# Moving the low halves of the first stream's cached values in a sample-attention loop

## The reference

```python
K = jnp.concatenate([prev_k, k], axis=1)      # 1024 cached + 16 new rows
V = jnp.concatenate([prev_v, v], axis=1)
F = jnp.cumsum(jnp.concatenate([prev_logf, logf], axis=1), axis=1)
s = einsum('bqhd,bkhd->bhqk', q, K) * scale + F_q - F_k
s = where(k_pos <= q_pos, s, -inf)
o = einsum('bhqk,bkhd->bqhd', softmax(s), V)
```

## Time and the profile before

| | |
|---|---|
| time of the runs | 1510.03 us median of 3 (1509.64 to 1511.13) |
| time of the profiled execution | 1514.69 us |
| its span | 1513.0 us |
| PE busy | 1474.3 us, 97% |
| DVE busy | 878.7 us, 58% |
| ACT busy | 616.2 us, 41% |
| POOL busy | 484.4 us, 32% |
| samples' attention | about 1161 to 1340 us of the span |

### The profile page before, as it was taken

How to read it: one execution, slowest core, us unless ns; L and a number is a source line. 1 busy time by engine, 2 the same in 40 slices (tenths; PEclk the granted TensorE clock), 3 DMA queues, 4 the chain that set the end, 5 groups by cost and what they waited for, 6 DMA issues and landing times.

```text
span 1513.0 us, 23830 instructions
## 1 busy us (share of the span) xinstructions
PE 1474.3 (97%) x8828; PEld 1310.5 (87%) x8828; DVE 878.7 (58%) x1883; ACT 616.2 (41%) x1307; POOL 484.4 (32%) x760
## 2 busy tenths in 40 slices
PE   8999999999999999999999999999998999999999
PEld 8997888888889999999888889889887788777887
DVE  4333103343364452321789888988986788798663
ACT  5443112131131110100578778777876444442220
POOL 2110004545540020102465665565573222103221
PEclk9999999999999999999999999999999899999999
DMA  5533114534330020160544853664433566644442
GB/s 165 157 110 100 44 67 127 167 112 143 94 105 27 22 68 20 42 137 24 123 100 83 144 119 65 128 134 81 97 98 129 186 227 229 242 141 151 156 160 91
DMA packets 180116, 174.48 MB, mean 115 GB/s; under 512 B 72543, under 2 KB 138240, under 8 KB 176928
## 3 DMA queue, kind: packets, MB, share of 16 engines
q1 hardware_dynamic: 177488, 163.97, 39.5%
q10 hardware_dynamic: 2448, 8.91, 1.5%
q0 software_dynamic: 64, 0.07, 0.1%
HBM read 123.27 MB, written 49.12 MB: 114 GB/s over the span
## 4 chain that ended last, share of the span: by engine, by line
PE 71%; DVE 9%; POOL 7%; issue 7%; ACT 5%; DMA 1%; DVEq 0%; ACTq 0%; POOLq 0%
PE banks L1069 19%; PE banks L1063 13%; PE banks L2690 7%; PE banks L1646 6%; PE banks L1662 4%; POOL in_h_rstd L589 3%; PE banks L1663 3%; PE banks L1636 3%; PE banks L1637 3%; PE banks L2139 3%; PE banks L2169 3%; POOL in_out L594 3%; ACT pa_s_ring L1528 2%; PE banks L2120 2%; DVE in_out L876 1%
## 5 line engine op out<-in xcount | busy, mean ns | idle before, releaser
L1063 PE MATMUL banks<-in_w_hi,in_xt_hi 128*128 128x512 f32 (+1 forms) x680 | 243.2, 358 | 4.3 <-DVE in_w_lo L767 2.5
L1063 PE MATMUL banks<-in_w_hi,in_xt_lo 128*128 128x512 f32 (+1 forms) x680 | 237.9, 350 | 0.0
L1063 PE MATMUL banks<-in_w_lo,in_xt_hi 128*128 128x512 f32 (+1 forms) x680 | 237.3, 349 | 0.0
L1608 DVE TENSOR_TENSOR pa_pt_lo<-banks,pa_pt_hi 128x512 fp32r<-128x512 f32 (+2 forms) x320 | 192.6, 606 | 20.1 <-ACT pa_pt_hi L1551 19.8
L1551 ACT ACTIVATE pa_pt_hi<-banks 128x512 fp32r<-128x512 f32 (+2 forms) x320 | 165.2, 537 | 86.8 <-PE banks L1646 86.5
L1069 PE MATMUL banks<-in_xt_hi,in_w_hi 128*128 128x384 f32 (+1 forms) x576 | 192.5, 334 | 0.9 <-DVE in_w_lo L773 0.7
L1069 PE MATMUL banks<-in_xt_hi,in_w_lo 128*128 128x384 f32 (+1 forms) x576 | 189.4, 329 | 0.0
L1069 PE MATMUL banks<-in_xt_lo,in_w_hi 128*128 128x384 f32 (+1 forms) x576 | 189.1, 328 | 0.0
L1646 PE MATMUL banks<-ident,pa_s_ring 128*128 128x128 f32 x1088 | 172.9, 274 | 12.6 <-ACT pa_s_ring L1528 7.2
L1528 ACT ACTIVATE pa_s_ring<-pa_s_ring,pa_low 128x1024 f32<-128x1024 f32 (+2 forms) x192 | 173.1, 902 | 0.1
L1662 PE MATMUL banks<-pa_pt_hi,pa_vs 128*128 128x256 f32 x576 | 165.2, 303 | 2.5 <-DVE pa_parts L1590 1.7
(11 more groups left out here) (293 smaller groups left out, 2872.3 us busy)
## 6 DMA issues: line engine op xcount, KB each, us to landing
sa_k_c<-in_cache_k_dram SPq DMA_DIRECT2D x8, 2048.0 KB, 9.8
sa_v_c<-in_cache_v_dram SPq DMA_DIRECT2D x8, 2048.0 KB, 9.4
out_dram<-in_out SPq DMA_DIRECT2D x34, 256.0 KB, 2.1
out_dram<-op_x ACTq DMA_DIRECT2D x17, 512.0 KB, 3.3
scratch_qk_t<-in_t_hi SPq DMA_DIRECT2D x32, 256.0 KB, 2.6
scratch_qk_t<-in_t_lo SPq DMA_DIRECT2D x32, 256.0 KB, 3.0
pa_q_l<-scratch_qk_t SPq DMA_DIRECT2D x16, 512.0 KB, 13.1
pa_ks<-scratch_qk_t SPq DMA_DIRECT2D x16, 512.0 KB, 6.3
```

Source lines behind the costliest of these rows:

```text
L1063: mm = pe.matmul(ps[:, u % NBANK, 0:n], tile_of(xa, t)[:, k, :], wa[:, k, c0:c0 + n], start=(k == 0 and q == 0), stop=(k == KT - 1 and q = ...
L1608: dve.tensor_tensor(pt_lo[g % 2][:, b:b + nb, cols], ps_t[:, turn_use(h, j, n) % 3, 0:nb * P].rearrange("p (b q) -> p b q", q=P), pt_hi[g ...
```

## The change

The four `low_v` calls of stream 0 leave their place behind the row minimum of stream 0. Two of them now stand in stream 1 behind the minimum of chunk 0, and two behind the minimum of chunk 1, each pair ahead of the `low_p(0)` that follows. The `low_v` of streams 1 to 7 stay where they were. ACT waits for the prompt's output stores before its first write of `p_hi`.

```diff
@@ sample_attention, on_act
         def high_p(b, part):
             for n in part:
                 tiles = PB[n]
+                if b == 0 and n == 0:
+                    prompt.stores_landed(act)
                 act.wait_ge(p_turned, b * 3 + n + 1)
@@ sample_attention, on_dve, the loop over streams
             low_k(b, 2)
             minima(b, par, 0)
+            if b == 1:
+                low_v(0, 0, 0)
+                low_v(0, 0, 1)
             if b:
                 low_p(b - 1, (0, 1))
             if b + 1 < NB:
                 low_k(b + 1, 0)
             minima(b, par, 1)
+            if b == 1:
+                low_v(0, 0, 2)
+                low_v(0, 0, 3)
             if b:
                 low_p(b - 1, (2,))
...
             dve.tensor_reduce(low[:, par, 3:4], low[:, par, 0:3], AX_X, ALU.min).then_inc(row_min, 1)
-            for quarter in range(4):
-                low_v(b, par, quarter)
+            if b:
+                for quarter in range(4):
+                    low_v(b, par, quarter)
```

## The result

The changed kernel takes 1530.07 us, median of 4 runs (1527.44 to 1530.75), beside 1510.58 us for the kernel before in its 4 runs (1509.64 to 1512.25). The ratio is 1.0112, 95% interval 1.0095 to 1.0129: slower by 17 us by the ratio, by 19.5 us by the medians. The forecast was 1524.5 us, +14.5 us, in a range of 1519.5 to 1528.5. (The ratio, put on the 1510.03 us from which the forecast started, gives 1526.9 us, inside it.) In another group of runs the same kernel took 1528.87 us against 1512.70 us, ratio 1.0103 (1.0090 to 1.0117), +16.2 us. The profiled executions differ by 16.0 us of span: 1529.0 us after, 1513.0 us before.

The account below looks back on a forecast made before the run. The prediction took PE, busy 97% of the span, to bound the kernel. It added 11.5 us of stall and 3.0 us of slow clock, 14.5 us, to 1510.03 us: 1524.5 us, range 1519.5 to 1528.5 us.

Parts of the forecast that it names:

- Removed from the end of stream 0: Taking the four subtractions from the end of stream 0 gains 0, as PE runs at its own pace there.
- The other bound: At full clock, PE's third group of transposes near 1187 would meet the old block; removing it gives 1.1 us.
- First pair: Two quarters behind the minimum of chunk 0 of stream 1 make `low_k` of stream 2 0.4 us late; PE loses 0.1 us.
- Second pair: Two quarters behind the minimum of chunk 1 of stream 1: PE waits 2.3 us more, counted at nothing because covered later.
- rival 2: Only the displaced DVE work counts: 2.3 us plus 1.4 us of clock, slower at 1513.7 us; chance 0.05.
- What the pair triggers: Stream 1's `load_v(1)` goes out late, DVE waits at `low_v(1)`, PE stalls in stream 2: +11.5 us, bounds 10.5 to 12.3.
- The clock: After PE's long stall in stream 2 the granted clock falls to half: 3.0 us taken, between 1.4 and 4.2.
- The sum: 11.5 + 3.0 = 14.5 us, worked on the profiled execution and put on the runs' 1510.03 us: 1524.5 us; chance 0.80.
- Queues: SP transfers behind `load_v` go out some 14 us later, forget sums maybe 1 us late; POOL's query halves later; nothing added.
- Later streams keep the shift: After stream 2 the delay neither shrinks nor grows: PE has no idle time, and the loop of the values moves whole.
- rival 4: Later loads take over 10.9 us, so five streams lose their 1.6 us of room: slower, 1529 us; chance 0.08.

Follow-up runs that it names:

- the gap filled: Kernel before, with 13 unread matmuls in PE's 2.51 us gap ahead of stream 1's scores: 1511.36 us, ratio 0.9994.
- late load alone: Kernel before, with the SP queue's load of stream 1's values also waiting for the minimum of chunk 1 of stream 1: 1526.43 us, ratio 1.0084.
- two stay: Changed kernel, with two quarters back at the end of stream 0 and two behind the minimum of chunk 0 of stream 1: 1520.12 us, ratio 1.0048.
- changed with the load halved: Changed kernel, each load of the values in two halves, after two and four quarters; POOL's split stays one instruction: 1526.18 us, ratio 1.0081.
- DVE work alone: Kernel before, with four extra DVE subtractions where the change puts the quarters; stream 0's own quarters stay: 1517.80 us, ratio 1.0038.
- four behind the first: Changed kernel, with all four quarters behind the minimum of chunk 0 of stream 1, none behind chunk 1's: 1522.45 us, ratio 1.0057.
- changed with fillers: Changed kernel, with 46 unread matmuls ahead of the PE transposes that wait 8.9 us in stream 2: 1527.51 us, ratio to before 1.0093.
- before with both halvings: Kernel before, with each load of the values in two halves and POOL's split in two instructions, gap not filled: 1512.22 us, ratio 0.9992.

## Why the prediction was right, and where its sum fell short

- **Removed from the end of stream 0: gain 0.** Right. DVE waits for ACT instead, and PE's pace is unchanged. The other bound, 1.1 us at full clock, is real: 0.94 us with the gap filled.
- **First pair: 0.1 us.** Off. PE waited 1.01 us at 1196.46, because the clock came back at about 1193 there and PE arrived earlier. It is covered by the later wait.
- **Second pair: 2.3 us more for PE, counted at nothing.** Right: PE's wait is 2.41 us, and it is covered. Alone, uncovered, the displaced work costs 5.0 us, against the 3.7 us at which rival 2 had it. POOL's split beside the second pair lengthened it by 0.9 us, and the first pair, priced at 0.1 us, made PE wait 1.92 us.
- **What the pair triggers: +11.5 us.** This is the mechanism, and it is shown by the late load alone, +13.6 us. Its size was +13.1. The term that was mis-sized is the time from issue to POOL's start: 10.28 us where 9.2 was taken from 8.98 and 9.42. The value came from the loads of streams 1 and 2 alone; those of streams 3 to 5 in the same trace take 10.05, 9.63 and 10.14 us (issues at 1226.69, 1246.04 and 1265.15, POOL's starts at 1236.74, 1255.67 and 1275.29). The bound was too low as well: it put the landing, at most 10.0 us, in the place of the time to POOL's start, but this landing took 10.13 us and POOL started 10.28 us behind the issue, so the +13.1 us of the term lie above its bound of 12.3. Then `low_v(1)` to `low_k` took 7.57 us (1215.67 to 1223.24) instead of 7.32, and the load went out 0.2 us later than worked out, as the second pair began 0.2 us later. 1.1 + 0.25 + 0.2 is the missing 1.6.
- **The clock: 3.0 us.** It was 3.0 in the profile (12.63 less 9.61), 2.25 us in the profile of the second measurement, and 1.4 us, with 0.4 lost to the fillers, when it was taken away. The mechanism was right. The size was a choice between 1.4 and 4.2, and that it met the first profile to a tenth is luck.
- **The sum.** 14.5 forecast, 16.0 between the profiled spans, 16.2 in the second group and 19.5 in the first, by medians. The prediction carried the sum of the profiled execution over to the median although that execution was 4.7 us above it. The changed kernel's profiled execution is only 0.7 us above its median. The remaining 3.5 us of the first group are thus in how far the profiled execution of before stood for its runs. The four runs of before in that group are also low: in the later groups, of 12 to 21 runs, its median is 1512.70 to 1513.36 us. Varying slow stretches are the likely reason, as their lengths at one place differ by 6.8 us between executions. The mean granted clock of the runs speaks for it: of the last group's 21 runs of before the fastest took 1510.25 us at 0.999 and the slowest 1516.64 us at 0.993, and a line through all 21 gives 0.75 us for each 0.001 of clock. For the first group's runs of before no clock is on record, so there it stays likely and not shown.
- **Queues.** The forget sums were up to 1.5 us late (1.53 us of PE's wait in the second measurement of the changed kernel, none in the first) and covered. The query halves on POOL were called harmless; they cost a little, as told below.
- **Later streams keep the shift.** Right: in the changed kernel the next two loads are issued 22.2 and 19.2 us apart (1220.62, 1242.82, 1262.05), and rival 4 did not come. (Its 10.0 us for "keys and values together" are in the earlier trace rows the loads of the values alone.)

## What to carry to other kernels

A reader of a single-buffered tile is also the gate of its next load. Before such a reader is moved into a stretch where its engine seems idle, follow the buffer from its last read on: issue, landing, each engine that works on it, and what stands behind the next reader in its list. Then compare the sum with the time that the kernel leaves for it. Here 21 to 22 us are needed of 22.98, so that a delay of 14 us came out nearly whole, on an engine that the moved work never touches. Take each term from all the loads in the trace that show it, not from two of them. When a filled gap or a removed hold-up gives nothing, look for the loop that takes over.

## What was not expected of the hardware

- **POOL and DVE slow each other.** While DVE's `low_v(1)` ran from 1215.67, POOL's small query operations took 1.12 to 1.18 us instead of 0.23 to 0.32 us, and DVE's block 4.92 us instead of 4.62. Two DVE subtractions beside POOL's split took 3.28 instead of 2.35 us. The Trainium skill (SBUF — State Buffer, SBUF: two separate sides) says that the two engines share a port pair, held exclusively for an instruction, also by a DVE operation with two SBUF inputs against a POOL operation that reads SBUF; by that rule, the traces agree. The slowed POOL operations take about as long as one of DVE's quarters, 1.2 us, and a pair of DVE that had to wait from 1198.16 to the end of POOL's split at 1199.24 would be 1.08 us late, where 0.93 were measured.
- **The same 2.5 us gap, two lengths of slow clock.** Eleven of the profiled executions have this gap of PE ahead of stream 1, and behind it the granted clock is 0.50 (1.2 GHz) with PE busy. It stays there for about 10.2 us in six of them (before and changed, both twice; two stay; changed with the load halved) and for about 3.4 us in five (DVE work alone, late load alone, four behind the first, changed with fillers, before with both halvings). The kernels do not sort them: the changed kernel with fillers is up to there the changed kernel.
- **A short wait can be enough, and a longer one can leave the clock alone.** In the kernel with the filled gap the clock fell behind a wait of 1.42 us and stayed at 0.50 to 1213.8, for 6.8 us. In the changed kernel it fell behind the wait of 2.41 us at 1202.42, and in its second measurement, behind 2.40 us at 1201.92, it stayed full.
- **The load's landing.** From issue to POOL's start it is 8.98 us in stream 1 of before and 10.28 us for the same 2 MB, issued 14 us later, though in both the keys follow on the queue about 3 us behind. The later loads of before take 9.42 to 10.14 us, and in its second execution the load of stream 2 takes 10.45, so 10.28 is within what other loads of this kernel show. The longest landing in any of the traces is 11.2 us. Why they differ is not settled.
